# Product-key routing of a two-block transformer: bfloat16 pairs for the comparisons, a later exponential, swapped one-hot comparisons

## Chip, cores and metric

One core of a Trainium2 chip runs the whole program. The metric is the device time in microseconds (us) of one execution. Three runs of the kernel before gave 1719.44, 1719.89 and 1723.61 us; the median, 1719.89 us, is the number that counts.

## What is computed

The reference sends 256 tokens of width 1024 through two blocks. The first holds differential attention, a gated convolution and two SwiGLU layers. The second holds an mLSTM and stick-breaking mixer, cross-attention over 256 memory tokens, and a PEER layer; only the PEER layer is touched here:

```python
s = einsum('thpc,hpnc->thpn', q, subkeys)          # 8 heads x 2 halves x 128 keys per token
s_top, i_top = top_k(s, 16)
cand = s_top[:, :, 0, :, None] + s_top[:, :, 1, None, :]
best, pos = top_k(cand, 16)                         # 16 of 256 pairs
experts = take_along_axis(i_top0 * 128 + i_top1, pos)
gates = softmax(best)
act = gelu(x . u[experts]) * gates ;  y = act . v[experts]
```

## The kernel before

The kernel computes the PEER layer densely: all 16384 experts are multiplied, and a gate matrix G (zero for experts that a token did not pick) weighs the results. Weights are split into a high and a low float32r part, and a product is three TensorE matmuls (high x high, low x high, high x low).

**Rows.** The expert-in stage is a loop over 128 rows, `for i in range(P)`, on each engine. A row is 128 experts. In row i:

- TensorE (`expert_in`, lines 1031 to 1033) does 24 matmuls of 128x256 with the weights uH and uL of row i. It first waits for uL(i).
- ScalarE (`usplit`, line 1591) copies uH(i + 2) from the raw weights. This waits until TensorE is through row i - 1, because there are three buffers. Then it may copy a batch of G (`gates`, line 1603), and then it applies Gelu to the row's result (line 1609), which waits for the end of row i on TensorE.
- The low part uL(i + 2) = raw - uH is made by VectorE for odd rows (line 2203, one instruction of 1024 columns) and by GpSimd for even rows (line 2459, four instructions of 256 columns).
- DMAs fetch raw weights into a ring of four buffers; a buffer comes free when its uH and uL are made. Gelu results go to a DRAM scratch.

After the 128 rows an expert-out stage (line 1066) does the second product in another 128 rows.

**Routing beside it.** VectorE finds the picks during the same rows. `route(j)` (j is one half of the tokens) is a generator of 49 steps. The plan written by `peer_plan` sets how many steps VectorE runs in each row: two in even rows and one in odd rows until the first half's picks are kept, one per row after that. In the numbers of the steps from 1:

- steps 1 to 34: the largest 16 of 128 for 16 rows of scores, 8 additions of candidates, the largest 16 of 256 for 8 heads (MAX8, FIND_INDEX8, MATCH_REPLACE8);
- step 35 (row 22 for j = 0, row 67 for j = 1): the subtraction of the maximum (line 2262, signal `s_cd`), then the wait for ScalarE's exponential (`s_gex`), the sum, the reciprocal and the gates (lines 2264 to 2270);
- step 36: the place of each pick is cut into two indices (lines 2273 to 2275) and each is cast to float32 (line 2279);
- steps 37, 39, 41 and again 43, 45, 47 for the second index: a comparison of 128 picks with 16 places (line 2287, 2048 columns, float32), a multiplication by the key numbers (line 2294, 2048 columns), and a sum over 16 (line 2299). `PAUSE` = 2 steps lie between them, so that the intermediate steps are empty.

ScalarE runs the exponential (line 1633) at the end of the row in which step 35 lies, after that row's Gelu. It needs another table than Gelu, so one table load stands before it and one before the next Gelu.

Then TensorE transposes the picks (`picks_turn`), VectorE keeps them (`picks_keep`, lines 2318 to 2327), and `hots(bt)` makes one-hot matrices for four tokens: oE (line 2347) and oB (line 2349) by comparisons of 512 columns in bfloat16 pairs, and three products oA (line 2352) that need oE. 64 batches of `hots` are spread over rows 36 to 121; TensorE multiplies each batch (`gates`, line 1020, 12 matmuls), and ScalarE copies the result to G.

In one row VectorE's order is: `usplit`, `picks_keep` if planned, the routing steps, `hots` if planned.

```python
            e.tensor_tensor(pairs(oE[n][:, :, :]), row, wide(i1T), ALU.is_equal).then_inc(s_dv, 1)
            t = next(own)
            e.tensor_tensor(pairs(oB[n][:, :, :]), row, wide(i2T), ALU.is_equal)
            e.wait_ge(s_dv, t)
            for i in range(3):
                r = e.tensor_tensor(pairs(oA[n][i][:, :, :]), pairs(oE[n][:, :, :]), wide(gp[i]), ALU.mult)
```

Of the kernel before, what the change touches and what calls it, by code (L numbers as in the profile page):

```python
# [9 lines left out]
BF16 = mybir.dt.bfloat16  # L10
F32R = mybir.dt.float32r
U32 = mybir.dt.uint32
ACT = mybir.ActivationFunctionType
AX = mybir.AxisListType.X

P = 128
# [17 lines left out]
PAUSE = 2  # L34
# [135 lines left out]
def build(nc, a, out, ctx):  # L170
    def sem(name):
        return ctx.enter_context(nc.semaphore(name))
# [3 lines left out]
    def sb(name, shape, dt=F32, off=None):  # L176
        size = int(np.prod(shape[1:])) * (2 if dt == BF16 else 4)
        size = -(-size // 32) * 32
        if off is None:
            off = at[0]  # L180
            at[0] += size
        else:
            o = off[0]
            off[0] += size
            assert off[0] <= nc.sbuf_usable_end, (name, off[0], nc.sbuf_usable_end)
            off = o
        return nc.alloc_sbuf_tensor_at(name, list(shape), dt, offset=off)
# [6 lines left out]
    xH = sb("xH", [P, KT, S], F32R)  # L194
    xL = sb("xL", [P, KT, S], F32R)
    ident = sb("ident", [P, P])
    iota = sb("iota", [P, P])
    mv = sb("mv", [P, 2, 4])
    rs = sb("rs", [P, 2, 4])
    eps = sb("eps", [P, 2])  # L200
# [11 lines left out]
    o = [OV]  # L212
# [26 lines left out]
    o = [OW]  # L239
# [79 lines left out]
    sc = sb("sc", [P, 2, 16, P], off=o)  # L319
    wk = [sb(f"wk{i}", [P, S], off=o) for i in range(4)]  # L320
    ti = sb("ti", [P, 16, 16], U32, off=o)
    tf = sb("tf", [P, 16, 16], off=o)
    tv = sb("tv", [P, 16, 16], off=o)
    bv = sb("bv", [P, 8, 16], off=o)
    bp = sb("bp", [P, 8, 16], U32, off=o)
    bq = [sb(f"bq{i}", [P, 8, 16], U32, off=o) for i in range(2)]
    bf = [sb(f"bf{i}", [P, 8, 16], off=o) for i in range(2)]
    ei = [sb(f"ei{i}", [P, 8, 16], off=o) for i in range(2)]
    gs = sb("gs", [P, 8, 2], off=o)
    eq = sb("eq", [P, P, 16], off=o)  # L330
    cand = sb("cand", [P, 8, S], off=[OW + 8192])
    o = [OG]
    ga = [sb(f"ga{i}", [P, S], off=o) for i in range(NA)]
# [21 lines left out]
    def flat2(x):  # L355
        return x.rearrange("p a b -> p (a b)")
# [5 lines left out]
    s_st = [sem(f"s_st{i}") for i in range(4)]  # L362
    s_rb = [sem(f"s_rb{i}") for i in range(4)]
    s_x = [sem(f"s_x{i}") for i in range(2)]
    (s_id, s_cst, s_lam, s_sub, s_memd, s_iota, s_cw, s_c4, s_gw, s_hs, s_gl, s_out) = (
        sem(n) for n in ("s_id", "s_cst", "s_lam", "s_sub", "s_memd", "s_iota", "s_cw", "s_c4", "s_gw", "s_hs", "s_gl", "s_out"))


    (s_used, s_tp, s_blk, s_row, s_qkp, s_sco, s_apt, s_avo, s_ojn, s_zc, s_gwm, s_gct, s_stl, s_sts, s_sto, s_ejn,
# [718 lines left out]
    def scalar(e):  # L1088
# [508 lines left out]
        def gates(bt):  # L1597
# [4 lines left out]
                e.wait_ge(s_hs, 16)  # L1602
            e.activation(G[:, j, :, t0:t0 + GB], ps[b][:, 0:GB * P].rearrange("p (t i) -> p i t", t=GB), ACT.Copy).then_inc(s_G, 1)

        def expert_in(i):
            e.wait_ge(s_ui, i + 1)
            if i >= 4:
                e.wait_ge(s_st[i % 4], 16 * (i // 4))
            e.activation(st[i % 4][:, :], ps[4 + i % 2][:, 0:S], ACT.Gelu).then_inc(s_ge, 1)  # L1609
# [11 lines left out]
        for i in range(P):  # L1621
            p = plan[i]
            usplit(i + US - 1)
            if i < 8:
                sub_scores(i // 4, i % 4)
            if p["gates"] is not None:
                gates(p["gates"])
            if i == P - 1:
                expert_act(0)
            expert_in(i)  # L1630
            if p["exp"] is not None:
                e.wait_ge(s_cd, p["exp"] + 1)
                e.activation(ei[0][:, :, :], ei[0][:, :, :], ACT.Exp).then_inc(s_gex, 1)
        expert_act(1)
        for i in range(P):
            usplit(P + i + US - 1)
# [21 lines left out]
    def vector(e):  # L1658
# [577 lines left out]
        def route(j):  # L2236
            for q in range(4):
                r = range(4 * q, 4 * q + 4)
                e.wait_ge(s_sc, 4 * j + q + 1)
                yield from top16([sc[:, j, x, :] for x in r], [wk[x % 4][:, 0:P] for x in r], [tv[:, x, :] for x in r],  # L2240
                                 [ti[:, x, :] for x in r], None)
            e.wait_ge(s_dv, top[0])
            e.tensor_copy(tf[:, :, :], ti[:, :, :]).then_inc(s_dv, 1)
            tf_t = next(own)
            s1 = tv[:, :, :].rearrange("p (h c) k -> p h c k", c=2)
            cv = cand[:, :, :].rearrange("p h (a b) -> p h a b", a=16)
            c_t = []
            e.wait_ge(s_sc, 8)
            for hd in range(8):
                e.tensor_tensor(cv[:, hd, :, :], s1[:, hd, 0, :].unsqueeze(2).broadcast_to([P, 16, 16]),  # L2250
                                s1[:, hd, 1, :].unsqueeze(1).broadcast_to([P, 16, 16]), ALU.add).then_inc(s_dv, 1)
                c_t.append(next(own))
                if hd % 2:
                    yield
            if j:
                e.wait_ge(s_pkp, j)
            for q in range(2):
                r = range(4 * q, 4 * q + 4)
                yield from top16([cand[:, x, :] for x in r], [wk[x % 4][:, :] for x in r], [bv[:, x, :] for x in r],
                                 [bp[:, x, :] for x in r], c_t[4 * q + 3])  # L2260
            e.wait_ge(s_dv, top[0])
            e.tensor_tensor(ei[0][:, :, :], bv[:, :, :], bv[:, :, 0:1].broadcast_to([P, 8, 16]), ALU.subtract).then_inc(s_cd, 1)
            e.wait_ge(s_gex, j + 1)
            e.reduce_sum(gs[:, :, 0], ei[0][:, :, :], AX).then_inc(s_dv, 1)
            t = next(own)
            e.wait_ge(s_dv, t)
            e.reciprocal(gs[:, :, 1], gs[:, :, 0]).then_inc(s_dv, 1)
            t = next(own)
            e.wait_ge(s_dv, t)
            e.tensor_tensor(bv[:, :, :], ei[0][:, :, :], gs[:, :, 1:2].broadcast_to([P, 8, 16]), ALU.mult).then_inc(s_dv, 1)  # L2270
            next(own)
            yield
            e.tensor_scalar(bq[0][:, :, :], bp[:, :, :], 4, None, ALU.logical_shift_right).then_inc(s_dv, 1)
            next(own)
            e.tensor_scalar(bq[1][:, :, :], bp[:, :, :], 15, None, ALU.bitwise_and).then_inc(s_dv, 1)
            t = next(own)
            e.wait_ge(s_dv, t)
            for i in range(2):
                e.tensor_copy(bf[i][:, :, :], bq[i][:, :, :]).then_inc(s_dv, 1)
                t = next(own)  # L2280
            yield
            tfv = tf[:, :, :].rearrange("p (h c) k -> p h c k", c=2)
            assert t > tf_t
            e.wait_ge(s_iota, 16)
            for i in range(2):
                e.wait_ge(s_dv, t)
                e.tensor_tensor(eq[:, :, :], flat2(bf[i][:, :, :]).unsqueeze(2).broadcast_to([P, P, 16]),
                                iota[:, 0:16].unsqueeze(1).broadcast_to([P, P, 16]), ALU.is_equal).then_inc(s_dv, 1)
                t = next(own)
                for _ in range(PAUSE):  # L2290
                    yield
                ev = eq[:, :, :].rearrange("p (h k) a -> p h k a", h=8)
                e.wait_ge(s_dv, t)
                e.tensor_tensor(ev, ev, tfv[:, :, i, :].unsqueeze(2).broadcast_to([P, 8, 16, 16]), ALU.mult).then_inc(s_dv, 1)
                t = next(own)
                for _ in range(PAUSE):
                    yield
                e.wait_ge(s_dv, t)
                r = e.reduce_sum(flat2(ei[i][:, :, :]), eq[:, :, :], AX)
                if i == 0:  # L2300
                    r.then_inc(s_dv, 1)
                    t = next(own)
                else:
                    r.then_inc(s_pk, 1)
                for _ in range(PAUSE):
                    yield
            yield

# [23 lines left out]
        def hots(bt):  # L2332
            n, tt = bt % 2, slice(GB * bt, GB * bt + GB)

            def wide(x):
                return x[:, tt, :].unsqueeze(2).broadcast_to([P, GB, P // 2, 2])

            def pairs(x):
                return x.rearrange("p t (a b) -> p t a b", b=2)

            row = pairs(iob[:, :].unsqueeze(1).broadcast_to([P, GB, P]))
            e.wait_ge(s_dv, sel[bt * GB // P])
            if bt == 0:
                e.wait_ge(s_iob, 1)
            if bt >= 2:
                e.wait_ge(s_gm, bt - 1)
            e.tensor_tensor(pairs(oE[n][:, :, :]), row, wide(i1T), ALU.is_equal).then_inc(s_dv, 1)
            t = next(own)
            e.tensor_tensor(pairs(oB[n][:, :, :]), row, wide(i2T), ALU.is_equal)
            e.wait_ge(s_dv, t)  # L2350
            for i in range(3):
                r = e.tensor_tensor(pairs(oA[n][i][:, :, :]), pairs(oE[n][:, :, :]), wide(gp[i]), ALU.mult)
            r.then_inc(s_hot, 1)
# [125 lines left out]
    def sync(e):  # L2479
# [15 lines left out]
        fetch(NR)  # L2495
        e.dma_start(cst[:, :], a["consts"]).then_inc(s_cst, 16)
        fetch(NR + 1)
        e.dma_start(iota[:, :], a["iota"]).then_inc(s_iota, 16)
        for n in range(NR + 2, NCH):
            fetch(n)  # L2500

# [160 lines left out]
```

## Time and profile before

| | us |
|---|---|
| median of three runs | 1719.89 |
| the profiled execution, its own time | 1719.99 |
| its span, first to last instruction | 1718.4 |
| TensorE busy | 1673.0 (97%) |
| VectorE busy | 1058.5 (62%) |
| ScalarE busy | 853.3 (50%) |
| GpSimd busy | 584.3 (34%) |

The expert-in rows lie between 925 and 1362 us of the span, the expert-out rows behind them. In the profile PE is TensorE's matmuls, DVE VectorE, ACT ScalarE, POOL GpSimd. Times are microseconds from the span's start. DVE and POOL instructions overlap a little at their ends, so the cost of one in a chain is the distance from its start to the next one's start. The mean granted clock of TensorE was 0.991.

### The profile page before, as it was taken

Reading aid. Unit: us, or ns where it says so; the run is one execution under the profiler, and the core shown is the slowest. Engines: PE = TensorE matmul, PEld = TensorE weight load, DVE = VectorE, ACT = ScalarE, POOL = GpSimd, SP = SyncE. Lnnn points to the kernel's source line nnn. Section 1 sums busy time; section 2 is a strip of 40 time slices with the busy share of each in tenths; the row PEclk is TensorE's granted clock in tenths of the full one; section 3 lists DMA queues with packets and bytes.
Section 4 is the critical chain, followed back from the end, with each engine's and each line's share of the span. In section 5 each row is a group of like instructions: output and inputs, shape, how many; then the busy total and the mean of one; then the engine's idle time right before and its main releaser. Section 6 shows DMA issues by size and latency. Waiting matters only on the chain.

```text
span 1718.4 us, 29521 instructions
## 1 busy us (share of the span) xinstructions
PE 1673.0 (97%) x11502; PEld 1525.1 (89%) x11502; DVE 1058.5 (62%) x1780; ACT 853.3 (50%) x1271; POOL 584.3 (34%) x727
## 2 busy tenths in 40 slices
PE   8989999999999999999999989999999999999998
PEld 6777999899899989877889989999999888888887
DVE  5566555476655546654254678899878455555555
ACT  5566445343544445565444444454455455445544
POOL 1666000030300015466602455657654422222221
PEclk9999999999999999999999999999999999999999
DMA  8334554554555555333344567666555677777775
GB/s 341 135 123 148 202 191 174 211 204 172 205 188 185 188 192 186 137 133 123 123 148 159 187 199 217 199 199 198 184 185 184 209 247 241 244 243 242 240 240 195
DMA packets 98363, 331.72 MB, mean 193 GB/s; under 512 B 11004, under 2 KB 44316, under 8 KB 79664
## 3 DMA queue, kind: packets, MB, share of 16 engines
q1 hardware_dynamic: 95904, 321.82, 55.3%
q0 software_dynamic: 2032, 6.89, 1.2%
q8 instruction: 92, 1.51, 0.4%
q10 hardware_dynamic: 288, 1.11, 0.2%
q14 instruction: 47, 0.39, 0.1%
HBM read 310.91 MB, written 18.87 MB: 192 GB/s over the span
## 4 chain that ended last, share of the span: by engine, by line
PE 87%; DVE 4%; ACT 3%; POOL 3%; DMA 1%; issue 1%; ACTq 0%; SPq 0%; DVEq 0%; POOLq 0%
PE banks L1066 20%; PE banks L525 10%; PE banks L451 8%; PE banks L452 8%; PE banks L453 8%; PE banks L1031 6%; PE banks L1032 6%; PE banks L1033 6%; PE banks L479 3%; POOL uL L2459 3%; PE banks L1020 2%; PE banks L508 1%; PE banks L441 1%; DMA raw<-in_qkv 1%; ACT wH L1102 1%
## 5 line engine op out<-in xcount | busy, mean ns | idle before, releaser
L2422 POOL TENSOR_TENSOR wL<-raw,wH 128x256 fp32r<-128x256 f32 x320 | 240.8, 789 | 557.5 <-ACT wH L1102 557.4
L2203 DVE TENSOR_TENSOR uL<-raw,uH 128x1024 fp32r<-128x1024 f32 x192 | 240.8, 1254 | 226.8 <-ACT uH L1591 226.6
L1591 ACT ACTIVATE uH<-raw 128x1024 fp32r<-128x1024 f32 x256 | 270.1, 1056 | 165.2 <-PE banks L1066 165.1
L451 PE MATMUL banks<-xH,wH 128*128 128x256 f32 x1168 | 329.7, 282 | 0.0
L452 PE MATMUL banks<-xL,wH 128*128 128x256 f32 x1168 | 329.2, 282 | 0.0
L453 PE MATMUL banks<-xH,wL 128*128 128x256 f32 x1168 | 328.7, 281 | 0.0
L2459 POOL TENSOR_TENSOR uL<-raw,uH 128x256 fp32r<-128x256 f32 x256 | 234.5, 946 | 260.1 <-ACT uH L1591 260.1
L1672 DVE TENSOR_TENSOR wL<-raw,wH 128x2048 fp32r<-128x2048 f32 (+1 forms) x101 | 229.1, 2273 | 137.4 <-ACT wH L1102 137.3
L1031 PE MATMUL banks<-xH,uH 128*128 128x256 f32 x1024 | 296.7, 290 | 9.6 <-POOL uL L2459 9.3
L1102 ACT ACTIVATE wH<-raw 128x2048 fp32r<-128x2048 f32 (+1 forms) x152 | 267.8, 1772 | 76.0 <-PE banks L525 68.5
L1032 PE MATMUL banks<-xL,uH 128*128 128x256 f32 x1024 | 289.9, 283 | 0.0
L1033 PE MATMUL banks<-xH,uL 128*128 128x256 f32 x1024 | 289.4, 283 | 0.0
L453 PEld LDWEIGHTS banks<-xH,wL 128*128 128x128 f32 x1168 | 220.1, 188 | 0.0
L452 PEld LDWEIGHTS banks<-xL,wH 128*128 128x128 f32 x1168 | 220.0, 188 | 0.0
L451 PEld LDWEIGHTS banks<-xH,wH 128*128 128x128 f32 x1168 | 219.9, 188 | 0.2
L1031 PEld LDWEIGHTS banks<-xH,uH 128*128 128x128 f32 x1024 | 194.6, 190 | 11.4 <-POOL uL L2459 11.3
L1032 PEld LDWEIGHTS banks<-xL,uH 128*128 128x128 f32 x1024 | 194.8, 190 | 0.0
L1033 PEld LDWEIGHTS banks<-xH,uL 128*128 128x128 f32 x1024 | 194.5, 190 | 0.0
L2468 POOL TENSOR_TENSOR ga<-st,G 128x256 f32<-128x256 f32 x128 | 98.9, 773 | 247.5 <-DVE gL L2359 235.9
L1609 ACT ACTIVATE st<-banks 128x256 f32<-128x256 f32 x128 | 49.2, 384 | 223.8 <-PE banks L1033 223.7
L1066 PE MATMUL banks<-uH,gH 128*128 128x512 f32 x504 | 155.7, 390 | 1.9 <-DVE gL L2359 1.9
L1066 PE MATMUL banks<-uH,gL 128*128 128x512 f32 x504 | 155.9, 391 | 0.0
(379 smaller groups left out, 2744.1 us busy)
## 6 DMA issues: line engine op xcount, KB each, us to landing
raw<-in_eu SPq DMA_DIRECT2D x128, 512.0 KB, 4.1
raw<-in_ev SPq DMA_DIRECT2D x128, 512.0 KB, 3.4
raw<-in_gu SPq DMA_DIRECT2D x44, 1024.0 KB, 4.7
raw<-in_dn SPq DMA_DIRECT2D x22, 1024.0 KB, 4.7
gelu_scratch<-st SPq DMA_DIRECT2D x128, 128.0 KB, 3.9
st<-gelu_scratch SPq DMA_DIRECT2D x128, 128.0 KB, 3.3
raw<-in_win SPq DMA_DIRECT2D x14, 1024.0 KB, 4.7
raw<-in_cin SPq DMA_DIRECT2D x12, 1024.0 KB, 4.8
```

The lines of the kernel that those rows point to most:

```text
L451: e.matmul(o, wh[:, w0:w0 + P], H[:, k, :], start=k == 0, stop=False)
L452: e.matmul(o, wh[:, w0:w0 + P], L[:, k, :], start=False, stop=False)
L453: t = e.matmul(o, wl[:, w0:w0 + P], H[:, k, :], start=False, stop=k == KT - 1)
L1031: e.matmul(ps[b][:, 0:S], wh[:, kc], xH[:, k, :], start=k == 0, stop=False)
L1032: e.matmul(ps[b][:, 0:S], wh[:, kc], xL[:, k, :], start=False, stop=False)
L1033: r = e.matmul(ps[b][:, 0:S], wl[:, kc], xH[:, k, :], start=False, stop=k == KT - 1)
L1066: r = e.matmul(ps[2 * t + q][:, :], l[i % NA][:, ts], w[:, q * 512:q * 512 + 512], start=i == 0 and m == 0, stop=False)
L1102: e.activation(wH[n % NS][:, c], raw[n % NR][:, c], ACT.Copy).then_inc(s_hi, 1)
L1591: e.activation(uH[n % US][:, :], raw[k // 2][:, (k % 2) * UW:(k % 2) * UW + UW], ACT.Copy).then_inc(s_uh, 1)
L2203: e.tensor_tensor(uL[n % US][:, :], raw[k // 2][:, (k % 2) * UW:(k % 2) * UW + UW], uH[n % US][:, :].bitcast(F32), ALU.subtract).then_inc( ...
L2422: r = e.tensor_tensor(wL[n % NS][:, d], raw[n % NR][:, d], wH[n % NS][:, d].bitcast(F32), ALU.subtract)
L2459: r = e.tensor_tensor(uL[n % US][:, d], raw[k // 2][:, (k % 2) * UW + c0:(k % 2) * UW + c0 + PW], uH[n % US][:, d].bitcast(F32), ALU.subtract)
```

## The change

Four edits in the routing:

1. The two indices of each pick are cast to bfloat16 and written twice side by side (`bf`, 256 columns instead of 128), the key numbers `tf` and the comparison's result `eq` become bfloat16, and the comparison reads pairs. The places 0 to 15 come from the bfloat16 tile `iob`, which GpSimd makes for the one-hots; the float32 tile `iota` and its DMA go.
2. On ScalarE the exponential of row r moves into row r + 1, behind that row's `usplit` and ahead of its G copy and its Gelu.
3. In `route` a `yield` comes in behind the subtraction: the wait for the exponential and all behind it come one step later. One of the two empty steps behind the last sum goes, so that there are 49 steps as before.
4. In `hots` oB comes ahead of oE.

```diff
-    iota = sb("iota", [P, P])
-    tf = sb("tf", [P, 16, 16], off=o)
+    tf = sb("tf", [P, 16, 16], BF16, off=o)
-    bf = [sb(f"bf{i}", [P, 8, 16], off=o) for i in range(2)]
+    bf = [sb(f"bf{i}", [P, P, 2], BF16, off=o) for i in range(2)]
-    eq = sb("eq", [P, P, 16], off=o)
+    eq = sb("eq", [P, P, 16], BF16, off=o)
...
+        def gate_exp(j):
+            e.wait_ge(s_cd, j + 1)
+            e.activation(ei[0][:, :, :], ei[0][:, :, :], ACT.Exp).then_inc(s_gex, 1)
...
             usplit(i + US - 1)
+            if i and plan[i - 1]["exp"] is not None:
+                gate_exp(plan[i - 1]["exp"])
...
             expert_in(i)
-            if p["exp"] is not None:
-                e.wait_ge(s_cd, p["exp"] + 1)
-                e.activation(ei[0][:, :, :], ei[0][:, :, :], ACT.Exp).then_inc(s_gex, 1)
...
             e.tensor_tensor(ei[0][:, :, :], bv[:, :, :], bv[:, :, 0:1].broadcast_to([P, 8, 16]), ALU.subtract).then_inc(s_cd, 1)
+            yield
             e.wait_ge(s_gex, j + 1)
...
-                e.tensor_copy(bf[i][:, :, :], bq[i][:, :, :]).then_inc(s_dv, 1)
+                e.tensor_copy(bf[i][:, :, :], flat2(bq[i][:, :, :]).unsqueeze(2).broadcast_to([P, P, 2])).then_inc(s_dv, 1)
...
-            e.wait_ge(s_iota, 16)
+            e.wait_ge(s_iob, 1)
...
-                e.tensor_tensor(eq[:, :, :], flat2(bf[i][:, :, :]).unsqueeze(2).broadcast_to([P, P, 16]),
-                                iota[:, 0:16].unsqueeze(1).broadcast_to([P, P, 16]), ALU.is_equal).then_inc(s_dv, 1)
+                e.tensor_tensor(eq[:, :, :].rearrange("p n (a b) -> p n a b", b=2), bf[i][:, :, :].unsqueeze(2).broadcast_to([P, P, 8, 2]),
+                                iob[:, 0:16].rearrange("p (a b) -> p a b", b=2).unsqueeze(1).broadcast_to([P, P, 8, 2]), ALU.is_equal).then_inc(s_dv, 1)
...
-                for _ in range(PAUSE):
+                for _ in range(PAUSE - i):
                     yield
...
+            e.tensor_tensor(pairs(oB[n][:, :, :]), row, wide(i2T), ALU.is_equal)
             e.tensor_tensor(pairs(oE[n][:, :, :]), row, wide(i1T), ALU.is_equal).then_inc(s_dv, 1)
             t = next(own)
-            e.tensor_tensor(pairs(oB[n][:, :, :]), row, wide(i2T), ALU.is_equal)
             e.wait_ge(s_dv, t)
...
-        e.dma_start(iota[:, :], a["iota"]).then_inc(s_iota, 16)
```

## Rows read from the trace of the kernel before

**Rows 1.** The page, part 4: shares by engine of the chain that ended last
```profile
PE 87%; DVE 4%; ACT 3%; POOL 3%; DMA 1%; issue 1%; ACTq 0%; SPq 0%; DVEq 0%; POOLq 0%
```

**Rows 2.** PE's waits, 960 to 1361 us: in total, times, longest (us)
```profile
PE banks L1031 <- POOL uL L2459: 6.8, 6, 4.5
```

**Rows 3.** Timeline of ACT, five Gelu starts (rows 7, 8, 89, 122, 126): start, length
```profile
959.72 0.38 ACT L1609 ACTIVATE st<-banks 128x256 f32<-128x256 f32 x1 [2.29 <-PE banks L1033]
...
962.57 0.38 ACT L1609 ACTIVATE st<-banks 128x256 f32<-128x256 f32 x1 [1.51 <-PE banks L1033]
...
1227.19 0.38 ACT L1609 ACTIVATE st<-banks 128x256 f32<-128x256 f32 x1 [1.77 <-PE banks L1033]
...
1345.55 0.38 ACT L1609 ACTIVATE st<-banks 128x256 f32<-128x256 f32 x1 [1.77 <-PE banks L1033]
...
1357.69 0.38 ACT L1609 ACTIVATE st<-banks 128x256 f32<-128x256 f32 x1 [1.52 <-PE banks L1033]
```

**Rows 4.** Timeline of PE, first matmul after a wait, [idle before <-releaser]
```profile
1015.45 0.58 PE L1031 MATMUL banks<-xH,uH 128*128 128x256 f32 x1 [4.51 <-POOL uL L2459]
...
1143.29 0.39 PE L1031 MATMUL banks<-xH,uH 128*128 128x256 f32 x1 [0.61 <-POOL uL L2459]
...
1163.61 0.39 PE L1031 MATMUL banks<-xH,uH 128*128 128x256 f32 x1 [0.75 <-POOL uL L2459]
```

**Rows 5.** Windows: PE, PEld, DVE, ACT, POOL busy us, PEclk, DMA share, GB/s
```profile
1016.00:1018.40 2.40, 2.40 (x14) 2.40 (x13) 0.46 (x1) 0.00 (x0) 2.16 (x4) 0.50 0.81 207
...
1125.00:1150.00 25.00, 24.39 (x229) 24.02 (x228) 24.62 (x70) 11.28 (x18) 14.57 (x16) 1.00 0.63 197
```

**Rows 6.** Timeline of ACT around the first exponential, rows 22 to 24
```profile
1002.44 0.38 ACT L1609 ACTIVATE st<-banks 128x256 f32<-128x256 f32 x1 [1.52 <-PE banks L1033]
1002.85 1.28 ACT L1633 ACT_TABLE_LOAD   x1
1004.14 0.31 ACT L1633 ACTIVATE ei<-ei 128x128 f32<-128x128 f32 x1
1004.36 1.04 ACT L1591 ACTIVATE uH<-raw 128x1024 fp32r<-128x1024 f32 x1
...
1006.71 0.39 ACT L1609 ACTIVATE st<-banks 128x256 f32<-128x256 f32 x1
1006.99 1.05 ACT L1591 ACTIVATE uH<-raw 128x1024 fp32r<-128x1024 f32 x1
```

**Rows 7.** Timeline of POOL: four undisturbed pieces, then single pieces
```profile
1001.00 2.87 POOL L2459 TENSOR_TENSOR uL<-raw,uH 128x256 fp32r<-128x256 f32 x4 [2.87 <-ACT uH L1591]
...
1008.12 2.20 POOL L2459 TENSOR_TENSOR uL<-raw,uH 128x256 fp32r<-128x256 f32 x1 [4.25 <-ACT uH L1591]
...
1014.68 0.72 POOL L2459 TENSOR_TENSOR uL<-raw,uH 128x256 fp32r<-128x256 f32 x1
...
1139.78 3.46 POOL L2459 TENSOR_TENSOR uL<-raw,uH 128x256 fp32r<-128x256 f32 x1
```

**Rows 8.** Timeline of DVE, 1004 to 1017 us
```profile
1004.48 0.29 DVE L2264 TENSOR_REDUCE gs<-ei 128x8 f32<-128x128 f32 x1 [1.90 <-ACT ei L1633]
...
1005.43 1.23 DVE L2203 TENSOR_TENSOR uL<-raw,uH 128x1024 fp32r<-128x1024 f32 x1
...
1007.43 2.29 DVE L2287 TENSOR_TENSOR eq<-bf,iota 128x2048 f32<-128x2048 f32 x1
1009.64 1.76 DVE L2203 TENSOR_TENSOR uL<-raw,uH 128x1024 fp32r<-128x1024 f32 x1
1011.33 2.81 DVE L2294 TENSOR_TENSOR eq<-eq,tf 128x2048 f32<-128x2048 f32 x1
1014.17 2.29 DVE L2299 TENSOR_REDUCE ei<-eq 128x128 f32<-128x2048 f32 x1
```

**Rows 9.** Timeline of DVE, a batch of one-hots and what follows, 1139.7 to 1142.6 us
```profile
1139.76 0.42 DVE L2347 TENSOR_TENSOR oE<-iob,i1T 128x512 bf16<-128x512 bf16 x1
...
1141.43 1.22 DVE L2203 TENSOR_TENSOR uL<-raw,uH 128x1024 fp32r<-128x1024 f32 x1
```

More of the change, by code:

```diff
@@ L364, in build @@
     s_x = [sem(f"s_x{i}") for i in range(2)]
-    (s_id, s_cst, s_lam, s_sub, s_memd, s_iota, s_cw, s_c4, s_gw, s_hs, s_gl, s_out) = (
-        sem(n) for n in ("s_id", "s_cst", "s_lam", "s_sub", "s_memd", "s_iota", "s_cw", "s_c4", "s_gw", "s_hs", "s_gl", "s_out"))
+    (s_id, s_cst, s_lam, s_sub, s_memd, s_cw, s_c4, s_gw, s_hs, s_gl, s_out) = (
+        sem(n) for n in ("s_id", "s_cst", "s_lam", "s_sub", "s_memd", "s_cw", "s_c4", "s_gw", "s_hs", "s_gl", "s_out"))
     (s_used, s_tp, s_blk, s_row, s_qkp, s_sco, s_apt, s_avo, s_ojn, s_zc, s_gwm, s_gct, s_stl, s_sts, s_sto, s_ejn,
```

## Prediction

> **What bounds the kernel now.** The chain of waits comes first: 87% of it is TensorE [rows 1]. So time is won only where TensorE pauses, and the change touches only the expert-in rows. PE's waits in that stage name one releaser, GpSimd's low part uL of an even row: 6.8 us idle in 6 times, the longest 4.5 [rows 2]. How much time the pauses cost in all follows from the Gelu starts [rows 3, 6], one per row: rows 8 to 22 take (1002.44 - 962.57) / 14 = 2.85 us each, rows 89 to 122, each with a batch of one-hots, (1345.55 - 1227.19) / 33 = 3.59. From row 7 to row 126 are 1357.69 - 959.72 = 397.97 us. Without pauses it would be 119 x 2.848 = 338.9, 64 batches x 0.739 = 47.3 and two transposes of 0.3: 386.8 or so. The pauses cost 11.1 us, and that is the most the change can win.
>
> More than half of it is one event. TensorE waits 4.51 us at 1015.45 [rows 4], and then runs at a granted clock of 0.50, the lower of the two levels (1.2 of 2.4 GHz), until 1018.4 [rows 5]. The time between Gelu starts there is 9.0 instead of 2.85: 6.2 us lost, of them 4.5 idle and 1.65 clock and restart. The other 4.9 us are short stalls between 1090 and 1225, which hold the other 2.3 us of the idle time [rows 2].
>
> **Where the long stall comes from.** Two things meet. ScalarE's Gelu of row 23 comes behind two table loads and the exponential, so that uH(26) is copied at 1006.99, 1.4 us late [rows 6]. Then GpSimd makes uL(26) in four pieces. Undisturbed they take 2.87 [rows 7]. Here the first alone takes 2.20, and all of uL(26) goes from 1008.12 to 1015.40. VectorE runs float32 instructions of two SBUF inputs then: the comparison (2.29), uL(27) (1.76 instead of 1.23), the multiplication (2.81 instead of 2.29) [rows 8]. So the two engines shut each other out: VectorE waits 0.53 for a GpSimd piece, and each piece waits for the whole VectorE instruction, ending about 0.7 behind it. The sum over 16 (2.29) shuts nothing out: the piece beside it takes 0.72 [rows 7, 8].
>
> A second pattern follows from the one-hots: in a batch, VectorE's five bfloat16 instructions start every (1141.43 - 1139.76) / 5 = 0.334 us, with uL directly behind [rows 9], and GpSimd's piece, asked for 0.02 us behind the first, takes 3.46: it gets in only after all six [rows 7]. TensorE pauses for 0.61 at 1143.29 [rows 4], and in the same manner near 1097.
>
> **Edit 1, pairs.** Two float32 instructions of 2048 columns cost 2.21 each from start to start, one of 1024 1.15 [rows 8], so some 0.1 fixed and 1.06 per 1024 columns. The one-hots do 512 bfloat16 columns in 0.334 [rows 9], so about 0.25 per 512, and 2048 cost 1.1. The access pattern of the comparison is that of the one-hots. The lower bound is 1.1, the upper 2.2 (no gain); I take 1.1. Eight instructions lose 1.1 each, 8.8 us of VectorE. That is not on the path; only the shorter shut-out is. The sums stay at 2.2 (at best 1.1), which is nothing, since GpSimd runs beside them. The casts go from 0.2 to at most 0.33 each. The DMA of `iota` goes from SP's queue at the start; no row shows anything waiting for it.
>
> **Edits 2 and 3, the exponential.** ScalarE now does, from 1002.7: uH(25) to 1003.8, load 1.28, exponential 0.31 to 1005.4, load, Gelu(23) at 1006.7. This is where it was, so uH(26) stays late and GpSimd still starts at 1008.1. What moves is VectorE: uL(25) is done by 1005.0 and no longer stands behind the sum. VectorE's wait for the exponential stays, and behind it now stand the routing steps (and in row 68 a batch of one-hots, which TensorE takes two rows later); nothing on TensorE waits for those in time.
>
> VectorE from there: sum, reciprocal, gates 0.95 [rows 8] from 1005.4 to 1006.4, cuts and casts 1.15 (0.85 before, 0.3 more for the width), comparison 1007.5 to 1008.6. GpSimd's first piece ends at 1009.3. VectorE's uL(27) (ready 1009.5) waits for the second until 1009.9 and runs until 1011.0; piece 3 ends at 1011.7; the multiplication, now in row 26 but directly behind, runs 1011.6 to 1012.7; piece 4 ends at 1013.4. Before it was 1015.4: 2.0 us less. The idle time is then 2.5 instead of 4.5. Such a pause probably still lowers the clock, so the 1.65 stays: the gain is 2.0, and 3.4 if the clock stays up.
>
> In the second half the long instructions fall in rows 70 to 78. One stall of 0.75 at 1163.61 [rows 4] and shorter ones to 1191 are from pieces shut out by 2.2 us instructions. Of the 4.9 us I give them, with restarts, 2.2; with 1.1 us instructions I expect 2.0 of that back (bounds 0 and 3.3, all that the next edit leaves).
>
> **Edit 4, the order of the one-hots.** oE is now directly ahead of the products that need it. VectorE has to wait for its own oE: the start of an instruction that waits so lies behind the end of the last one instead of 0.08 ahead of it (0.42 long, 0.334 apart) [rows 9], about 0.12 us. That is 64 x 0.12 = 7.7 us of VectorE over 86 rows, in its idle time. In the gap nobody holds the way to SBUF, and GpSimd, which stood outside for 3.46, gets in after two instructions. I take the stalls at 1097 and 1143 as gone: 1.6 us with restarts (bounds: 0, and 2.4 with the stalls near 1215, of which I take 0.3). Against it: once GpSimd is in, each of VectorE's products waits 0.53, and the first half's second index may meet a new stall, 0.3.
>
> The Trainium skill's page "SBUF — State Buffer" (section "SBUF: two separate sides") says that VectorE and GpSimd share a pair of ports under an exclusive lock, held for a whole instruction by whoever starts first. The rows of the comparison agree; the piece of 3.46 does not, since by that rule it would have been let in after 0.33. By the rule alone edit 4 would win nothing.
>
> **Sum.** 2.0 + 2.0 + 1.6 + 0.3 - 0.3 = 5.6 us off the profiled execution's 1719.99, which is 0.1 above the median: 1714.4 us. The expert-out rows start so much earlier and stay as they are. A measurement of this kernel can tell about 0.3%, 5.2 us, from no change, so the forecast lies just beyond that.
>
> **Rivals.**
> - *The clock stays up in row 26*: the idle time of 2.5 lies between 4.51, behind which it fell, and 0.61, the pause at 1143.29, whose window keeps 1.00 [rows 4, 5]. 1.4 us more: 1713.0. Chance 0.15.
> - *GpSimd stays shut out in the one-hots*, because a gap of 0.12 us is too short for it, or because it never depended on the gap. For it: it did not get in between six instructions [rows 7, 9]. Then edit 4 wins nothing: 1719.99 - 4.0 = 1716.0. Chance 0.20. This is also the time by the skill's rule above.
> - *The pairs don't run faster* (the change doesn't do what it says). For it: the row of the same pattern has an inner run of 128, here 16. Both gains of 2.0 go: 1718.4. Chance 0.09.
> - *VectorE becomes the bound*: slower. It was busy 24.62 of 25 us from 1125 to 1150 [rows 5]. Two rows take 2.85 + 3.59 = 6.44. VectorE's share of them is uL 1.15, one-hots 1.8, two steps of the 256-wide search about 3.0: 5.9. If each of GpSimd's four pieces, now let in, costs it 0.53, it is 8.0, and it falls behind by 1.6 in each of five such pairs and by 0.5 in eight pairs before: 12 us. Some 3.8 of that are slack, the rest is lost as stalls for odd uL: 8 - 2 = 6 us slower, 1726. It decides once most batches meet a piece. Against it: TensorE did not wait for VectorE once in the stage [rows 2], and the pieces that are let in sooner are the ones that VectorE used to meet later. Chance 0.06.
>
> **Chances.** The forecast itself 0.48, its own range 1712.5 to 1716.5; 0.02 for anything else. It is faster by over 0.3% in about 0.7 of the forecast's cases, in all of the first rival's, and in 0.15 of the second's: 0.52. Slower 0.06. The rest, 0.42, is within 0.3%. The range reaches from 1711.0, the clock up and the terms at their better bounds, to 1718.6, which takes in the pairs that don't run faster.
>
> **What the changed profile would show.** If right: the wait of TensorE near 1015 is 2 to 3 us, with the clock at 0.50 behind it; comparisons and multiplications of 2048 bfloat16 columns at 1.2; uL(26) by GpSimd in 5.3 instead of 7.3; no piece above 3 us in the rows 36 to 80; Gelu(23) where it was. Wrong would be: long instructions above 2; pieces of over 3 us beside a batch of one-hots; waits of TensorE for line 2203; a stall in row 26 of 4 us, or none at all, which would mean that the late uH(26) is not what I take it for.

## The result, and the profile after

| | before | after |
|---|---|---|
| median of five executions, us | 1719.89 (1716.76 to 1724.44) | 1712.46 (1709.54 to 1715.26) |
| the profiled execution, its own time | 1719.99 | 1713.52 |
| its span | 1718.4 | 1712.1 |
| Gelu of row 7 to Gelu of row 126 | 397.97 | 392.62 |

The ratio of the executions is 0.9945, 95% interval 0.9924 to 0.9967: faster by 0.55%. On the median of before that is 1710.4 us (1706.8 to 1714.2), below the range that was given (1711.0 to 1718.6). The miss is narrow: the median of after, 1712.46, lies inside the range, the direction was as forecast, and the profiled executions differ by 6.5 us, close to the 5.6 of the forecast. The changed kernel, timed again on another chip, was at 0.9934 (0.9917 to 0.9951), median 1712.2. So some 10 us were won by the ratios, and the profiles show 6.

TensorE's wait for uL in the same stretch of the stage [rows 2], and the Gelu starts that bound it [rows 3]:

```profile
PE banks L1031 <- POOL uL L2463: 2.6, 2, 2.1
```
```profile
959.52 0.38 ACT L1613 ACTIVATE st<-banks 128x256 f32<-128x256 f32 x1 [2.33 <-PE banks L1033]
...
1352.14 0.39 ACT L1613 ACTIVATE st<-banks 128x256 f32<-128x256 f32 x1 [1.52 <-PE banks L1033]
```

Six waits of 6.8 us have become two of 2.6. The two are the one in row 26, 2.06 instead of 4.51 [rows 4], and a new one in row 30. Those at 1143.29 and 1163.61 have no successor. PE's timeline:

```profile
1013.38 0.39 PE L1031 MATMUL banks<-xH,uH 128*128 128x256 f32 x1 [2.06 <-POOL uL L2463]
...
1027.11 0.38 PE L1031 MATMUL banks<-xH,uH 128*128 128x256 f32 x1 [0.58 <-POOL uL L2463]
```

The timelines of ACT, DVE and POOL around the first exponential [rows 6, 8, 7]. The numbers of the lines differ by a few from kernel to kernel (L2463 here is L2459 of the kernel before):

```profile
1004.07 1.28 ACT L1607 ACT_TABLE_LOAD   x1
1005.36 0.31 ACT L1607 ACTIVATE ei<-ei 128x128 f32<-128x128 f32 x1
1005.69 1.28 ACT L1613 ACT_TABLE_LOAD   x1
1006.98 0.39 ACT L1613 ACTIVATE st<-banks 128x256 f32<-128x256 f32 x1
1007.26 1.05 ACT L1591 ACTIVATE uH<-raw 128x1024 fp32r<-128x1024 f32 x1
```
```profile
1007.46 1.22 DVE L2291 TENSOR_TENSOR eq<-bf,iob 128x2048 bf16<-128x2048 bf16 x1
1009.84 1.23 DVE L2206 TENSOR_TENSOR uL<-raw,uH 128x1024 fp32r<-128x1024 f32 x1 [1.16 <-ACT uH L1591]
1010.99 1.75 DVE L2298 TENSOR_TENSOR eq<-eq,tf 128x2048 bf16<-128x2048 bf16 x1
```
```profile
1008.39 4.93 POOL L2463 TENSOR_TENSOR uL<-raw,uH 128x256 fp32r<-128x256 f32 x4 [4.27 <-ACT uH L1591]
```

Gelu of row 23 and the copy behind it stand where they stood, against a row 22 that is 0.28 later in this execution. The comparison takes 1.22 instead of 2.29, the multiplication 1.75 with 0.54 of waiting for a piece in it, and the four pieces 4.93 instead of 7.28. That is the walk of the prediction, almost to the tenth. What it did not contain was found by the experiments.

### The profile page after: what moved, and what is told of

Same layout as the page of the kernel before. It is cut to its first block, busy times and chain, and to the rows that moved or that the text cites. A ratio compares the mean times of both kernels' runs of the same rounds, so it can differ in the third digit from the quotient of the medians.

```text
span 1712.1 us, 29520 instructions
## 1 busy us (share of the span) xinstructions
PE 1672.8 (98%) x11502; PEld 1525.9 (89%) x11502; DVE 1065.1 (62%) x1780; ACT 853.2 (50%) x1271; POOL 562.1 (33%) x727
## 4 chain that ended last, share of the span: by engine, by line
PE 86%; DVE 7%; ACT 3%; DMA 1%; issue 1%; POOL 1%; ACTq 0%; DVEq 0%; POOLq 0%
PE banks L1066 20%; PE banks L525 10%; PE banks L451 8%; PE banks L453 8%; PE banks L452 8%; PE banks L1031 6%; PE banks L1032 6%; PE banks L1033 6%; PE banks L479 3%; PE banks L1020 2%; PE banks L508 2%; DMA raw<-in_qkv 1%; PE banks L441 1%; DVE oA L2356 1%; POOL uL L2463 1%
## 5 line engine op out<-in xcount | busy, mean ns | idle before, releaser
L2206 DVE TENSOR_TENSOR uL<-raw,uH 128x1024 fp32r<-128x1024 f32 x192 | 237.0, 1234 | 212.4 <-ACT uH L1591 212.3
L2463 POOL TENSOR_TENSOR uL<-raw,uH 128x256 fp32r<-128x256 f32 x256 | 209.4, 848 | 279.2 <-ACT uH L1591 279.2
```

Of the source, the lines that this page charges most:

```text
L2206: e.tensor_tensor(uL[n % US][:, :], raw[k // 2][:, (k % 2) * UW:(k % 2) * UW + UW], uH[n % US][:, :].bitcast(F32), ALU.subtract).then_inc( ...
```

## The experiments

The row numbers are those of the stage's loop, and a row takes 2.85 us, or 3.59 with a batch of one-hots, where TensorE waits for nothing. In every experiment the ratio is against the kernel before on the same chip, and "stage" is Gelu 7 to Gelu 126 in the profiled execution (before 397.97, after 392.62 and 391.14).

### The four edits, one by one

**The swap alone** (e1).

```diff
+            e.tensor_tensor(pairs(oB[n][:, :, :]), row, wide(i2T), ALU.is_equal)
             e.tensor_tensor(pairs(oE[n][:, :, :]), row, wide(i1T), ALU.is_equal).then_inc(s_dv, 1)
             t = next(own)
-            e.tensor_tensor(pairs(oB[n][:, :, :]), row, wide(i2T), ALU.is_equal)
```

> The kernel before with oB ahead of oE alone. Theory (the wait for its own oE opens a gap in which GpSimd gets in): the stall of 4.5 us near 1015 stays, the stalls near 1097 and 1143 go, no GpSimd piece in rows 36 to 80 that stands beside one-hots alone lasts over 2 us (before 3.5), and the time falls by 2 us (1.5 to 3). Rival (GpSimd stays shut out for a whole batch): pieces of 3 us and both stalls stay, no change of the time. Rival (VectorE becomes the bound): TensorE waits for VectorE's line of uL, slower by 2 us or more.

Ratio 0.9961 (0.9947 to 0.9974). The stage takes 397.18 us, 0.8 less than before: the stalls near 1097 and 1143 are gone, and smaller ones in rows 86 and 88 (0.8 us together) too, but others in rows 78, 83 and 87 are 1.3 us larger or new, and rows 8 to 22 ran at 2.88 instead of 2.85. The one in row 83 is a wait for VectorE:

```profile
1201.87 0.34 PE L1020 MATMUL banks<-oA,oB 128*128 128x128 bf16 x3 [0.67 <-DVE oA L2352]
```

So the profiles differ by 0.8, the timed executions by nearly 7, where the expectation had 2.

**The old order with the same gap** (e4): the products wait for oB too.

```diff
-            e.tensor_tensor(pairs(oB[n][:, :, :]), row, wide(i2T), ALU.is_equal)
+            e.tensor_tensor(pairs(oB[n][:, :, :]), row, wide(i2T), ALU.is_equal).then_inc(s_dv, 1)
+            t = next(own)
             e.wait_ge(s_dv, t)
```

> The kernel before with its own order of the one-hots (oE, oB), but the products wait for oB as well, so that the gap lies in the same place as with the swap. Theory (the gap is what lets GpSimd in): the same as the swap alone, stalls near 1097 and 1143 gone, 2 us faster, within 0.7 us of it in the expert-in stage. Rival (the order of the two comparisons does it, not the gap): stalls as before, no change.

Ratio 0.9954 (0.9939 to 0.9970), stage 396.94, the same stalls gone. The batch that shut a piece out for 3.46 [rows 7, 9] is here, DVE and POOL:

```profile
1142.45 0.42 DVE L2347 TENSOR_TENSOR oE<-iob,i1T 128x512 bf16<-128x512 bf16 x1
1142.77 0.43 DVE L2349 TENSOR_TENSOR oB<-iob,i2T 128x512 bf16<-128x512 bf16 x1
1143.24 1.51 DVE L2353 TENSOR_TENSOR oA<-oE,gp 128x512 bf16<-128x512 bf16 x3
```
```profile
1142.47 1.33 POOL L2460 TENSOR_TENSOR uL<-raw,uH 128x256 fp32r<-128x256 f32 x1
```

The third line starts 0.04 us behind the end of the second (1142.77 + 0.43) instead of 0.08 ahead of it, and the piece is let in there: 1.33 instead of 3.46. The piece was asked for 0.02 us behind oE, as before. With the swap alone it is 1.33 too, at 1147.02. It is the gap, and the order only makes it. Row 83 waits 0.69 for VectorE's oA here too.

**The pairs alone** (e3: the changed kernel with the old exponential and the old order).

> The kernel before with the bfloat16 pairs alone. Theory (a piece waits for a whole VectorE instruction, so shorter ones shut GpSimd out for less): wait in row 26 of 2.7 us instead of 4.5, the stalls between 1157 and 1191 gone, those near 1097 and 1143 (one-hots) as before: 4 us faster (3 to 5). Rival (the late start of uL(26) is what counts): the wait in row 26 stays above 4 us, under 2 us faster.

Ratio 0.9934 (0.9916 to 0.9952), stage 391.71. The wait in row 26:

```profile
1011.65 0.39 PE L1031 MATMUL banks<-xH,uH 128*128 128x256 f32 x1 [2.52 <-POOL uL L2459]
```

The stalls of 0.75 and less between 1157 and 1191 are gone, those at the one-hots of 0.47 and 0.59 are there, with a piece of 3.46. This edit alone wins as much as all four together. The stage is 6.3 us shorter, more than the 3 to 5 expected, because the clock stayed up in row 26 (5.64 us between Gelu starts for a wait of 2.52).

**The later exponential alone** (e2).

```diff
+            if i and plan[i - 1]["exp"] is not None:
+                gate_exp(plan[i - 1]["exp"])
...
-            if p["exp"] is not None:
-                e.wait_ge(s_cd, p["exp"] + 1)
-                e.activation(ei[0][:, :, :], ei[0][:, :, :], ACT.Exp).then_inc(s_gex, 1)
...
+            yield
             e.wait_ge(s_gex, j + 1)
...
-                for _ in range(PAUSE):
+                for _ in range(PAUSE - i):
```

> The kernel before with the exponential one row later on ScalarE and the extra step in route alone. Theory (Gelu of row 23 still stands behind two table loads, uH(26) is as late as before): uL(26) starts and ends within 0.5 us of before, TensorE waits 4 to 5 us in row 26, time within 1 us of before. Rival (the place of the exponential is what made the stall): the wait in row 26 falls by 1.6 us or more, to under 3.

Neither came: it is slower, ratio 1.0032 (1.0014 to 1.0050), stage 412.42. TensorE's wait in row 26 is as the theory said (4.03), but two other stalls are new, in rows 30 and 78. PE and POOL of this kernel:

```profile
1031.49 0.58 PE L1031 MATMUL banks<-xH,uH 128*128 128x256 f32 x1 [3.68 <-POOL uL L2463]
...
1194.63 0.58 PE L1031 MATMUL banks<-xH,uH 128*128 128x256 f32 x1 [5.92 <-POOL uL L2463]
```
```profile
1183.73 8.80 POOL L2463 TENSOR_TENSOR uL<-raw,uH 128x256 fp32r<-128x256 f32 x1 [3.43 <-ACT uH L1591]
```

One piece that takes 0.72 undisturbed was shut out for 8 us. Row 78 took 11.4 us instead of 3.3, and row 30 9.0 instead of 2.9. I had held that GpSimd gets in behind a long VectorE instruction in any case. It does not.

### The changed kernel with parts undone

**Without the swap** (e5: order oE, oB).

> The changed kernel with the one-hots' old order (oE, oB): pairs and the later exponential stay. With the exponential alone one GpSimd piece was shut out for 8.8 us in row 78, because the comparison, the one-hots, uL and the multiplication stood in one chain without a gap. Theory (only the gap in the one-hots breaks that chain): here it is 2.3 us shorter, so a piece of 5 to 7 us and a stall of 2 to 4 us in row 78, 3 to 6 us slower than the changed kernel. Rival (the pairs alone take the harm out of the later exponential): no piece above 4 us, at most 2 us slower than the changed kernel.

Ratio 0.9952 (0.9935 to 0.9969), median 1716.02 against 1712.20 of the changed kernel beside it: 3.8 us, the theory's size. The profile shows less: a wait of 1.50 in row 78, behind a piece of 2.4, and the stalls of the one-hots, in a stage of 393.82. The theory's piece of 5 to 7 us is not there, so in the profiled execution the pairs alone take most of the harm away, as the rival has it. But it is also the fastest of the five, 1712.25, and the others took 1715.3 to 1716.4; whether those hold a longer shut-out is not shown. The intervals of the two ratios overlap.

**Without the later exponential** (e6: pairs and swap).

> The changed kernel with the exponential and the steps of route where they were before: pairs and the swap stay. Theory (the later exponential only moves the long instructions, and costs the stall of 0.8 us in row 30): rows 7 to 126 take 390 us, 2 to 3 less than the changed kernel, with a wait in row 26 of 2.5 us and none in row 30. Rival (the three edits help each other): the changed kernel is faster by 1 us or more.

Ratio 0.9920 (0.9902 to 0.9938), median 1710.46. No wait in row 30, and 2.42 in row 26, as the theory has it. But the stage took 393.22, not 390: behind the 2.42 the granted clock fell to 0.54 for 3.5 us (7.06 us for the row), and in row 87 TensorE waited 0.67 for VectorE's oA. The median is 1.7 us under the changed kernel's, the two intervals overlap. The rival (the changed kernel faster by 1 us) has nothing for it; that this one is the faster is not settled.

**The first half's exponential one row later still** (e7).

```diff
-            if i and plan[i - 1]["exp"] is not None:
-                gate_exp(plan[i - 1]["exp"])
+            for j, late in ((0, 2), (1, 1)):
+                if i >= late and plan[i - late]["exp"] == j:
+                    gate_exp(j)
...
-            yield
+            for _ in range(2 - j):
+                yield
...
-                for _ in range(PAUSE - i):
+                for _ in range(PAUSE - i * (2 - j)):
```

> The changed kernel with the first half's exponential yet one row later (row 24), so that the copy that the table loads delay is uH(27), whose low part is VectorE's single instruction, and not uH(26), whose low part is GpSimd's four pieces; the routing's later steps of that half follow by one step. Theory (the stall in row 26 comes from a late uH of an even row together with the shut-out): no wait in row 26, clock at full there, rows 7 to 126 take 388 to 389.5 us, 3 to 4.5 less than the changed kernel. Rival (the shut-out by long instructions is enough): a wait of 1.5 us or more in rows 24 to 30.

Ratio 0.9916 (0.9899 to 0.9934), median 1709.09, stage 388.93. Timelines of ACT and POOL:

```profile
1004.84 1.05 ACT L1591 ACTIVATE uH<-raw 128x1024 fp32r<-128x1024 f32 x1
1005.91 1.28 ACT L1607 ACT_TABLE_LOAD   x1
```
```profile
1005.97 2.81 POOL L2465 TENSOR_TENSOR uL<-raw,uH 128x256 fp32r<-128x256 f32 x4 [2.82 <-ACT uH L1591]
```

uH(26) is copied ahead of the table load, its four pieces take 2.81 undisturbed, and row 26 has no wait. A smaller one stands in row 28, where the pieces of uL(28) meet the comparison and the multiplication:

```profile
1017.23 0.39 PE L1031 MATMUL banks<-xH,uH 128*128 128x256 f32 x1 [1.31 <-POOL uL L2465]
```

The copy uH(28) is not late, so the shut-out alone makes a stall of 1.31, near the 1.5 that the rival asked for. The late copy of an even row adds the rest of the 2.06. This version has the lowest median of all, 3.1 us under the changed kernel's beside it, with intervals that overlap.

**The changed kernel again** (e8).

> The changed kernel itself on the same chip, as the measure for the other three: rows 7 to 126 in 392.6 us, give or take 0.5 for the pace of rows 8 to 22, and 0.993 to 0.996 of the kernel before.

Ratio 0.9934 (0.9917 to 0.9951). The stage took 391.14, 1.5 less than in the first profile and outside the 0.5 that was allowed, and this is a clock matter: rows 26 and 27 took 6.54 and 2.98 us there and 5.18 and 2.85 here. In both the wait in row 26 is 2.06 us. Windows behind it, of the first profile and then of this one (columns as in [rows 5], PEclk is the third from the end):

```profile
1014.50:1018.00 3.50, 3.50 (x19) 3.50 (x19) 0.00 (x0) 0.11 (x1) 1.59 (x3) 0.52 0.91 318
```
```profile
1011.60:1016.00 4.40, 4.37 (x36) 4.37 (x37) 0.00 (x0) 1.22 (x2) 2.75 (x4) 1.00 0.78 235
```

### Where 5 us are that no profile had shown

Beside the first eight experiments the kernel before was mostly near 1725 us, and its one profiled execution had taken 1720. The two are called its upper and its lower level here. It was profiled three times more, unchanged (e9, e10, e11).

> The kernel before, unchanged, profiled again. In 46 runs beside the experiments it took 1718 to 1733 us, most near 1726, while its profiled execution took 1720. Theory (whether a GpSimd piece gets in during a chain of VectorE instructions is not fixed, and most executions have a long shut-out that the profiled one lacks): an execution above 1724 us shows in rows 7 to 126 over 402 us, with a piece above 5 us and a stall of 3 us or more between 1140 and 1230. Rival (the difference lies elsewhere, in the clock or the transfers): rows 7 to 126 within 2 us of 398, the difference outside them.

> The same kernel once more, for the same question: if it takes 1717 to 1721 us, rows 7 to 126 take 396 to 400 us and no piece is above 4 us; if above 1724, as in the run before it.

> The same kernel a third time, for the same question and with the same two expectations.

They took 1719.76, 1718.64 and 1720.39 us, with stages of 397.85, 399.44 and 397.84 and no piece above 3.7: the lower level each time. The one execution beside them without a profile took 1723.99. So none of the three could show what the upper level holds.

The next four localise it by opening the gap in part of the rows of the kernel before.

```diff
-            e.tensor_tensor(pairs(oB[n][:, :, :]), row, wide(i2T), ALU.is_equal)
+            r = e.tensor_tensor(pairs(oB[n][:, :, :]), row, wide(i2T), ALU.is_equal)
+            if bt < 15:
+                r.then_inc(s_dv, 1)
+                t = next(own)
             e.wait_ge(s_dv, t)
```

That is e12; the condition is `15 <= bt < 23` in e13 and `bt >= 23` in e14.

> The kernel before with the gap in the one-hot batches of rows 36 to 64 only (15 of 64). Every profiled execution of the kernel before takes 1718.6 to 1720.4 us, most others 1724 to 1729, and the gap in all batches won 8 us over those where the profiles differ by 1. Theory (the other executions have a shut-out in rows 66 to 80 that the profiled ones lack, as the kernel with the exponential alone shows one in row 78): 1 to 2 us faster, its other executions still near 1725. Rival (it lies in rows 36 to 64): median at 1718 to 1720, ratio under 0.997.

> The same with the gap in the batches of rows 66 to 80 only (8 of 64), beside the long instructions of the second half. Theory: this is where it lies, the median falls by 5 to 7 us against the kernel before, to 1718 to 1720, and executions near 1726 are gone, while the profile is within 1 us of before. Rival (it lies elsewhere): within 2 us of the kernel before, executions of 1725 as before.

> The same with the gap in the batches of rows 81 to 121 only (41 of 64). Theory: under 2 us faster than before, executions near 1725 as before. Rival (it lies behind row 80, where every row has a batch): median at 1718 to 1720.

In e15 the one-hots are as before, and the first half's comparisons and multiplications wait for `expert_low` of the last uL that VectorE made.

> The kernel before with its own order of the one-hots, and the comparisons and multiplications of the first half waiting for the low part uL that VectorE made last, so that a gap stands between the two. There are no one-hots yet. Theory: no change, the pieces beside them already get in between; row 26 stays at 9 us, executions near 1725 as before. Rival (the missing 6 us lie in rows 24 to 31 of the executions that are not profiled): median 5 us or more below the kernel before.

```
                     ratio (95%)                  executions, us                       above 1723
before               -                            1716.6 to 1728.1, median 1723.2      18 of 35
e12 rows 36 to 64    0.9989 (0.9967 to 1.0012)    1714.0 to 1727.4, median 1725.0       7 of 12
e13 rows 66 to 80    0.9979 (0.9964 to 0.9994)    1715.1 to 1724.4, median 1719.0       1 of 12
e14 rows 81 to 121   0.9998 (0.9979 to 1.0018)    1715.8 to 1727.5, median 1723.2       6 of 12
e15 first half       1.0007 (0.9988 to 1.0026)    1717.2 to 1729.5, median 1725.0       7 of 12
```

With the gap in the eight batches of rows 66 to 80, 1 of 12 executions is above 1723, against 38 of the other 71: only these batches take the upper level away. The median falls by 4.2 us, where 5 to 7 was expected. e12 and e14 were expected to be up to 2 us faster, and are not told from the kernel before. Two profiled executions, of e12 and of e15, fell on the upper level: 1725.0 and 1726.2 us of span, stages of 405.21 and 406.23. Both show the same stall in row 78. In e15, where nothing there differs from the kernel before:

```profile
1190.68 0.58 PE L1031 MATMUL banks<-xH,uH 128*128 128x256 f32 x1 [6.26 <-POOL uL L2468]
```
```profile
1179.43 9.15 POOL L2468 TENSOR_TENSOR uL<-raw,uH 128x256 fp32r<-128x256 f32 x1 [3.08 <-ACT uH L1591]
```
```profile
1177.90 1.21 DVE L2204 TENSOR_TENSOR uL<-raw,uH 128x1024 fp32r<-128x1024 f32 x1
1179.04 2.28 DVE L2295 TENSOR_TENSOR eq<-bf,iota 128x2048 f32<-128x2048 f32 x1
1181.24 0.41 DVE L2356 TENSOR_TENSOR oE<-iob,i1T 128x512 bf16<-128x512 bf16 x1
...
1184.05 2.28 DVE L2303 TENSOR_TENSOR eq<-eq,tf 128x2048 f32<-128x2048 f32 x1
...
1186.93 1.08 DVE L2361 TENSOR_TENSOR oA<-oE,gp 128x512 bf16<-128x512 bf16 x3
```

Fourteen VectorE instructions from uL on follow each other, none with a gap, and the piece asked for 0.39 us into the comparison gets in behind the last. In e12 the piece takes 8.79 and TensorE waits 5.89. In the profile of before the same chain with the same piece, asked for 0.41 us into the comparison, goes the other way, POOL and DVE:

```profile
1178.61 2.47 POOL L2459 TENSOR_TENSOR uL<-raw,uH 128x256 fp32r<-128x256 f32 x1 [3.09 <-ACT uH L1591]
```
```profile
1178.20 2.28 DVE L2287 TENSOR_TENSOR eq<-bf,iota 128x2048 f32<-128x2048 f32 x1
1180.41 0.95 DVE L2347 TENSOR_TENSOR oE<-iob,i1T 128x512 bf16<-128x512 bf16 x1
```

Here the piece is let in behind the comparison, oE waits for it (0.95 instead of 0.41), and from then on the two take turns. Row 78 takes 3.3 us in the one case and 11.4 in the other. The rest of the stage makes up for little of it: stalls in rows 80, 86 and 88 are smaller by 1.0 us together. Rows 26 and 27 are 1.3 us longer in e15, by the clock behind a wait of the same length. In all five profiled executions whose rows 66 to 80 are as before and which fell on the lower level (before, e9, e10, e11, e14) the piece takes 2.45 to 2.47. So the same instructions go the one way or the other from execution to execution.

## Why the prediction was right and wrong

**Right.** The bound: the stage loses 11.1 us to waits for GpSimd's uL, and VectorE is not waited for. The pairs run at the lower bound taken (1.1 from start to start), the sums stay at 2.28. Gelu(23) does not move. Row 26: wait 2.06 where 2.5 was said, 2.4 us less than before where 2.0 was said; the clock fell behind it in one profile, which was the forecast, and stayed in the other, which was the first rival. The stalls from 1157 to 1191: gone, 2.2 us with restarts, of which 2.0 was taken. The stalls of the one-hots: gone by the gap (e4), 1.6 us as taken. The new stall in row 30 costs 0.84 (3.69 instead of 2.85) where 0.3 was taken. By the profiles the stage is 5.35 and 6.8 us shorter, where 5.6 was said. The second rival (GpSimd stays shut out) is refuted by e1 and e4, the third by the 1.22, the fourth by a VectorE that was busy 22.6 of 25 us from 1125 to 1150 instead of 24.62, and never waited for in the changed kernel's stage. In e1, e4, e6 and e14 it was, once each, for 0.7 us, so there was something to that rival's cost.

**Wrong: the step "Sum", where the profiled execution's 1719.99 stood for the kernel because it was "0.1 above the median".** The kernel before has two levels some 7 us apart, and the five executions' median fell on the lower by chance (two of the five are at 1723.6 and 1724.4). Beside the experiments 50 of 76 executions were above 1723, 13 below 1720 and 13 between, so the levels are blurred. The term that was missing is a shut-out of 8 to 9 us in row 78, 8.1 us lost in that row (11.4 against 3.3) and some 7 in the whole, in about half or more of the executions. From the lower level alone the forecast of 5.6 would have been close: the profiled executions differ by 6.5. The changed kernel was at 1709.5 to 1715.3 in all eleven timed ones. The upper level is taken away by the gap (e13), and perhaps by the pairs (all eight of e3 are at 1711.8 to 1716.9, though the chain in row 78 has no gap there); in the changed kernel both are at work.

**And the step "Edit 4"**, which gave it 1.6 us with 2.4 as the upper bound. Alone it won 0.39%, 6.7 us (e1). It reckoned with the trains that the one profile had, not with a train that goes through the one-hots, uL and the long instructions. In the prediction's own rows was a hint: the piece of 3.46 was let in neither behind oE nor behind any of the next four, while at 1008.12 one came in behind the first. A behaviour with two outcomes in one profile can have two outcomes in one place. The bound should have come from the chain without a gap: from the start of the comparison, beside which the piece is asked for, 2.2 + 1.7 + 1.15 + 2.2 + 1.7 = 9 us. That sum is made after the fact, but from rows that were there.

**Edits 2 and 3** were costed at nothing. With float32 comparisons they cost 0.32% (e2): row 30 loses 6.1 us behind a wait of 3.68, and all ten executions are at 1729 or above, the profiled one with the stall in row 78. With the pairs this shrinks to the 0.84 in row 30; e6 without them is not slower.

By the Trainium skill's page "SBUF — State Buffer", section "SBUF: two separate sides", whichever of the two engines starts first gets the shared pair of ports for the whole instruction, and the other is blocked. The prediction took this to mean that a waiting piece is let in behind the instruction in progress, and that edit 4 would then win nothing. The pieces of 8.80 and 9.15 us, shut out over twelve instructions behind the first, refute that reading. They don't contradict the sentence itself, which leaves open who gets the pair next.

What stays open: what tips the balance in row 78. The offset of the request (0.39 and 0.41 us) doesn't tell the cases apart. In e12 the two groups of executions (1714.0 to 1715.3, and 1724.9 to 1727.4) lie 11 us apart, more than the 7 that the stall explains. And e3 and e5, which have no gap in their one-hots, spread over 4 to 5 us, with the profiled execution the fastest of each, so a shorter shut-out in the others is possible. Nor could it be shown that the timed executions near 1725 have the stall, since these carry no profile; that e13 alone removes all but one of them, and that both profiles on that level have the stall, is the evidence.

## What to carry to other kernels

Where VectorE and GpSimd both work on SBUF beside each other, look for chains of VectorE instructions with two SBUF inputs and no gap: here a GpSimd instruction was held up by the rest of such a chain, and not only by the longest instruction. A wait for VectorE's own result in its middle is cheap (0.12 us here) and ends the chain. Take the before of a comparison from many executions: a profile is one draw, and where the times have two levels, find the wait that only one of them has. Where a stall has two causes, as a late copy and a shut-out here, either can be taken away, and the cheaper one may be to let the delay fall on another row; what the other cause does alone (1.31 us in row 28) stays.

## What the runs showed of the hardware

- A GpSimd instruction that takes 0.72 us undisturbed took up to 9.15 us (e15) beside VectorE instructions that follow each other without a gap, each of them with two SBUF inputs. In the same place it took 2.47 in other executions. Once in, the engines take turns, at 0.54 us a turn for VectorE.
- A gap of 0.04 us between two VectorE instructions let it in every time that was looked at: in e1, e4 and the changed kernel no piece in the stage is above 2.8, 2.8 and 1.7 us, and none beside one-hots alone above 1.5.
- After two waits of equal length, 2.06 us, in the same row of the same kernel, TensorE's granted clock fell to about half for 3.5 us in one execution and stayed at 1.00 in the other. It stayed up behind a wait of 2.52 (e3) and fell behind one of 2.42 (e6). That is worth about 1.5 us a time (6.54 and 2.98 us for rows 26 and 27 against 5.18 and 2.85).
